# The FFN's first product as seven products of quarters instead of eight

## What is computed

```python
def merge_and_ffn(x, o_attn, o_rwkv, o_fnet, mod, p):
    ...
    x = x + g1 * o
    h = modulate(rmsnorm(x, p['norm_ffn_g']), sh2, sc2)
    gt, up = jnp.split(h @ p['ffn_w_in'], 2, axis=-1)       # (640, 1024) @ (1024, 5632)
    return x + g2 * ((jax.nn.silu(gt) * up) @ p['ffn_w_out'])  # (640, 2816) @ (2816, 1024)
```

## Time and profile before

| | us |
|---|---|
| median of three runs (2017.24 to 2019.22) | 2018.57 |
| the profiled execution | 2016.91 |
| its span, first to last instruction | 2015.1 |
| PE busy | 1912.3 (95%) |
| DVE busy | 804.5 (40%) |
| ACT busy | 634.6 (31%) |
| POOL busy | 517.1 (26%) |
| granted TensorE clock, mean | 0.987 |

### The profile page before, as it was taken

One profiled execution on the slowest core, in us unless ns is written; L12 is line 12 of the kernel. 1 busy time (PEld: TensorE's weight loads), 2 busy tenths in 40 slices (PEclk: granted clock), 3 DMA queues, 4 the chain that ended last, 5 costly groups with the idle time before them and its releaser, 6 DMA issues. The chain is left out here.

```text
span 2015.1 us, 47947 instructions
## 1 busy us (share of the span) xinstructions
PE 1912.3 (95%) x21577; PEld 1789.0 (89%) x21577; DVE 804.5 (40%) x1740; ACT 634.6 (31%) x1254; POOL 517.1 (26%) x251
## 2 busy tenths in 40 slices
PE   5999899899999999999999988989999999999997
PEld 4998588788899999999989866869888999999997
DVE  0522866554243311333153257474525332133322
ACT  3422555552321211212233155455323221111221
POOL 0333400001233333333312340001032333333331
PEclk8999899999999999999999998999999999999999
DMA  9575200002532232222336522000021222332221
GB/s 332 165 203 162 64 4 4 4 5 85 153 100 63 58 99 76 73 71 66 90 102 196 173 67 65 4 2 7 24 64 48 78 64 73 84 84 66 59 65 53
DMA packets 238176, 164.09 MB, mean 81 GB/s; under 512 B 21643, under 2 KB 235381, under 8 KB 237461
## 3 DMA queue, kind: packets, MB, share of 16 engines
q1 hardware_dynamic: 236532, 159.07, 27.1%
q0 software_dynamic: 1440, 1.97, 0.3%
HBM read 157.87 MB, written 3.15 MB: 80 GB/s over the span
## 5 line engine op out<-in xcount | busy, mean ns | idle before, releaser
L669 POOL TENSOR_TENSOR wsplit<-ring,wsplit 128x1024 fp32r<-128x1024 f32 (+1 forms) x134 | 355.4, 2653 | 795.5 <-ACT wsplit L1386 795.5
L873 PE MATMUL PS<-h_hi,wsplit 128*128 128x320 f32 x1408 | 425.6, 310 | 4.4 <-POOL wsplit L669 2.6
L874 PE MATMUL PS<-h_hi,wsplit 128*128 128x320 f32 x1408 | 423.8, 309 | 0.0
L1386 ACT ACTIVATE wsplit<-ring 128x1024 fp32r<-128x1024 f32 (+1 forms) x134 | 152.2, 1136 | 792.2 <-PE PS L874 779.9
L873 PEld LDWEIGHTS PS<-h_hi,wsplit 128*128 128x128 f32 x1408 | 264.2, 188 | 9.1 <-ACT h_hi L1360 4.3
L874 PEld LDWEIGHTS PS<-h_hi,wsplit 128*128 128x128 f32 x1408 | 264.4, 188 | 0.0
L874 PE MATMUL PS<-h_lo,wsplit 128*128 128x320 f32 x704 | 217.1, 309 | 0.0
L873 PE MATMUL PS<-h_lo,wsplit 128*128 128x320 f32 x704 | 217.1, 309 | 0.0
L873 PE MATMUL PS<-hid_hi,wsplit 128*128 128x320 f32 x704 | 213.1, 311 | 0.0
L874 PE MATMUL PS<-hid_hi,wsplit 128*128 128x320 f32 x704 | 212.0, 309 | 0.0
L2032 DVE SCALAR_TENSOR_TENSOR x<-PS,mod,x 128x320 f32<-128x320 f32 x144 | 54.5, 434 | 343.9 <-PE PS L874 343.9
(11 more groups left out here) (383 smaller groups left out, 3728.2 us busy)
## 6 DMA issues: line engine op xcount, KB each, us to landing
ring<-in_w_ada SPq DMA_DIRECT2D x48, 1024.0 KB, 7.6
ring<-in_ffn_w_in SPq DMA_DIRECT2D x88, 512.0 KB, 5.1
ring<-in_ffn_w_out SPq DMA_DIRECT2D x32, 704.0 KB, 4.6
ring<-in_w_in SPq DMA_DIRECT2D x8, 1024.0 KB, 7.4
ring<-in_w_in SPq DMA_DIRECT2D x10, 512.0 KB, 8.8
ring<-in_w_in SPq DMA_DIRECT2D x16, 256.0 KB, 6.5
ring<-in_w_out SPq DMA_DIRECT2D x16, 256.0 KB, 6.8
ring<-in_w_out SPq DMA_DIRECT2D x8, 512.0 KB, 8.0
```

The lines of the kernel that those rows point to most:

```text
L669: nc.gpsimd.tensor_tensor(lo, raw_w, hi, SUB).then_inc(wl_ready(), 1)
L873: mm(lat[:, 0:TH], w, v[:, 0:TH], start=(n == 0), stop=(n == total - 1))
L874: last = mm(cx[:, 0:TH], w, v[:, TH:T], start=(n == 0), stop=(n == total - 1))
L1386: act(hi, raw_w, ACT.Copy).then_inc(wh_ready(), 1)
```

## The change

The first FFN product of one tile is a matrix of 2 x 2 blocks times another: the weights are cut by input half (k-tiles 0 to 3, 4 to 7) and by output (gate, up), h by input half and by tokens (left 320, right 320). The plain way is eight products of quarters, 12 matmuls each. The change makes them by Strassen's algorithm in the Winograd form, seven products of sums of quarters, named by their weight block in the order of computation: A11, A12, S2, S1, S3, S4, A22 (S1 to S4 are sums of the tile's weight blocks). All that is done for 20 of the 22 tiles of a layer (`NFAST`); the first two remain plain.

- The sums of h's quarters (in `h` itself, once a layer) and their high and low parts (`T_hi`, `T_lo`): 4 DVE sums, 4 ACT copies, 4 DVE subtractions of 128 x 1280; and ACT first completes `h` (16 instructions).
- For each fast tile: DVE makes 4 sums of weight blocks (128 x 512), ACT the high part of 7 blocks, DVE the low part of 6, POOL that of A22. There are five slots for blocks: ACT makes the high part five products ahead, DVE the low part four ahead.
- Products gather in PSUM: A11, then S2, S3 and A22 on top of it in a bank of the tile's own (6 or 7); A12 in bank 5, then S1, S4 on top of S1 in the same bank. Between them ACT copies three states out and DVE adds three and multiplies one.
- The FFN is done in four parts of 6, 6, 5, 5 tiles instead of two of 11. An f2 unit is 36 or 30 matmuls; there are 32 a layer instead of 16; its weights come as 256 columns for two units, in three slots.
- The third unit's weights (`FFN0 + 2`) are split with no wait for PE, into `wsplit`.
- SP's load of the last gain waits for the last of the seven-product tiles.
- Buffers lie over others to make room: `Sf` over the recurrence's state, `E4` (which holds `tmp` too) over small tables.

The core of the diff:

```diff
+PARTS = ((0, 6), (6, 12), (12, 17), (17, 22))
+NPLAIN = 2
...
@@ SP
+                    elif old[0] == "f1" and old[1] >= NPLAIN:
+                        e.wait_ge(bl_ready.sem, bl_ready.upto(lo, 6 * (old[1] - NPLAIN + 1)))
+                        e.wait_ge(bp_ready.sem, bp_ready.upto(lo, old[1] - NPLAIN + 1))
...
-            e.wait_ge(acc_ready.sem, acc_ready.upto(DEPTH - 1, ITEM_AT[("up", FT - 1)] + 1))
+            e.wait_ge(sp_done.sem, sp_done.upto(DEPTH - 1, 7 * NFAST))
             e.dma_start(grow, I["norm_final_g"].partition_broadcast(128)).then_inc(ld_grow, 16)
...
@@ POOL
+                for part in range(len(PARTS)):
+                    for si in fast_pairs(part):
+                        n, hi, lo = fast_slot(si, A22)
+                        e.wait_ge(bh_ready.sem, bh_ready.upto(l, 7 * si + A22 + 1))
+                        nc.gpsimd.tensor_tensor(lo, fast_raw(l, si, A22)[1], hi, SUB).then_inc(bp_ready(), 1)
+                    for m in range(KT):
+                        weight_low(UNIT_OF[("f2", m, part)])
...
@@ PE
+                def product(si, q):
+                    n, w_hi, w_lo = fast_slot(si, q)
+                    v_hi, v_lo, _ = fast_in(q)
+                    bank = ps[5] if q in (A12, S1_, S4_) else ps[6 + si % 2]
...
+                    if q == A12 and si >= 1:
+                        e.wait_ge(ps_taken.sem, ps_taken.upto(l, 4 * (si - 1) + 3))
+                    if q in (S2_, S3_, S4_):
+                        e.wait_ge(ps_copied.sem, ps_copied.upto(l, 3 * si + {S2_: 1, S3_: 2, S4_: 3}[q]))
+                    if q in (S1_, A22):
+                        e.wait_ge(ps_taken.sem, ps_taken.upto(l, 4 * si + {S1_: 1, A22: 2}[q]))
+                    for k in range(4):
+                        for p in range(3):
+                            last = mm(bank[:, 0:TH], (w_lo if p == 1 else w_hi)[:, k, :],
+                                      (v_lo if p == 2 else v_hi)[:, k, :],
...
@@ ACT
+                weight_high(FFN0 + 2)
+                for k in range(KT):
+                    e.wait_ge(hl_ready.sem, hl_ready.upto(l, KT + k + 1))
+                    for s, (a, b) in enumerate(STREAMS):
+                        last = act(h[:, k, a:b], h[:, k, a:b], ACT.Identity, bias=mod[:, 24 + k, s:s + 1])
+                    last.then_inc(h_full(), 1)
...
+                    for si in fast_pairs(part):
+                        ends = si == fast_pairs(part)[-1]
+                        own_x, tile = ps[6 + si % 2], si + NPLAIN - PARTS[part][0]
+                        e.wait_ge(hid_split.sem, hid_split.upto(l, max(NPLAIN, si + 1)))
+                        product_copy(si, A11, E1[si % 2], own_x)
+                        block_ahead(si, A11, 5)
+                        block_ahead(si, A12, 5)
+                        left_or_right_sigmoid(si, 1, E1[si % 2])
+                        e.wait_ge(hid_split.sem, hid_split.upto(l, NPLAIN + si))
+                        product_copy(si, S2_, E2, own_x)
+                        block_ahead(si, S2_, 5)
+                        product_copy(si, S1_, G5[:, :], ps[5])
+                        block_ahead(si, S1_, 5)
+                        if ends:
+                            weight_high(f2)
+                        block_ahead(si, S3_, 5)
+                        block_ahead(si, S4_, 5)
+                        left_or_right_sigmoid(si, 3, E2)
+                        block_ahead(si, A22, 5)
+                        e.wait_ge(ps_taken.sem, ps_taken.upto(l, 4 * si + 4))
+                        act(hid_hi[:, tile, 0:TH], E1[si % 2], ACT.Copy)
+                        e.wait_ge(right_ready.sem, right_ready.upto(l, si + 1))
+                        act(hid_hi[:, tile, TH:T], E2, ACT.Copy).then_inc(hid_high(), 1)
...
@@ DVE
+                def block_low(si, q):
+                    if q == A11:
+                        weight_sum(si, S1_)
+                        weight_sum(si, S2_)
+                    if q == S3_:
+                        weight_sum(si, S4_)
+                    n, hi, lo = fast_slot(si, q)
+                    e.wait_ge(bh_ready.sem, bh_ready.upto(l, 7 * si + q + 1))
+                    V.tensor_tensor(lo, fast_raw(l, si, q)[1], hi, SUB).then_inc(bl_ready(), 1)
+                    if q == S1_:
+                        weight_sum(si, S3_)
...
+                for k in range(KT):
+                    e.wait_ge(h_full.sem, h_full.upto(l, k + 1))
+                    if k == 3:
+                        input_sum(quarter(0, 0), quarter(0, 1), quarter(0, 0))
+                        plain_gate(0)
+                input_sum(quarter(0, 1), quarter(1, 1), quarter(0, 1))
+                plain_up(0)
+                input_sum(quarter(1, 1), quarter(1, 1), quarter(0, 0))
+                input_sum(quarter(1, 0), quarter(1, 0), quarter(1, 1))
+                block_low(0, 0)
+                sum_low(S2_)
+                sum_low(S1_)
+                block_low(0, 1)
+                block_low(0, 2)
+                plain_gate(1)
+                sum_low(S3_)
+                sum_low(A22)
+                plain_up(1)
+                block_low(0, 3)
+                for part in range(len(PARTS)):
+                    for si in fast_pairs(part):
+                        own_x, tile = ps[6 + si % 2], si + NPLAIN - PARTS[part][0]
+                        left = E1[si % 2]
+                        if si > fast_pairs(part)[0]:
+                            pair_low(si - 1, tile - 1)
+                        low_ahead(si, A11)
+                        e.wait_ge(ps_copied.sem, ps_copied.upto(l, 3 * si + 1))
+                        product_sum(si, A12, left, ps[5], ADD)
+                        low_ahead(si, A12)
+                        e.wait_ge(g_sig.sem, g_sig.upto(l, 2 * si + 1))
+                        own.after(V.tensor_tensor(left, left, F4, MUL))
+                        low_ahead(si, S2_)
+                        low_ahead(si, S1_)
+                        e.wait_ge(ps_copied.sem, ps_copied.upto(l, 3 * si + 3))
+                        product_sum(si, S3_, G5[:, :], own_x, ADD)
+                        low_ahead(si, S3_)
+                        product_sum(si, S4_, E2, ps[5], ADD)
+                        low_ahead(si, S4_)
+                        e.wait_ge(g_sig.sem, g_sig.upto(l, 2 * si + 2))
+                        own.after(V.tensor_tensor(E2, E2, F4, MUL))
+                        product_sum(si, A22, left, own_x, MUL)
+                        V.tensor_tensor(E2, E2, G5[:, :], MUL).then_inc(right_ready(), 1)
+                        low_ahead(si, A22)
+                    pair_low(si, tile)
+                    for m in range(KT):
+                        residual(("f2", m, part), m, 40, TH)
```

More of the change, by code:

```diff
@@ L54, in chunk_order @@
         ffn = []
[L55 to L56 removed]
+        for part, (a, b) in enumerate(PARTS):
+            ffn += [(l, "f1", i) for i in range(a, b)] + [(l, "f2", 4 * part + m) for m in range(KT // 2)]
         order += ffn[:1] + ahead[6:] + ffn[1:]
@@ L88, in split_units @@
     u += [(("out", m), ("wo", m // 2), m % 2, KT) for m in range(KT)]
[L89 to L92, removed]
+    for i in range(NPLAIN):
+        u += [(("gate", i), ("f1", i), 0, KT), (("up", i), ("f1", i), 1, KT)]
+    for part, (a, b) in enumerate(PARTS):
+        u += [(("f2", m, part), ("f2", 4 * part + m // 2), m % 2, b - a) for m in range(KT)]
     return u
@@ L120, in item_order @@
     o += [("out", m) for m in range(KT)] + [("inv", 1)]
[L121 to L124, removed]
+    for i in range(NPLAIN):
+        o += [("gate", i), ("up", i)]
+    for part in range(len(PARTS)):
+        o += [("f2", m, part) for m in range(KT)]
     return o
@@ L217, in state_plan, with fast_pairs, part_of @@
     return plan
+A11, A12, S2_, S1_, S3_, S4_, A22 = range(7)
+T_AT = {S2_: 0, S1_: 1, S3_: 2, A22: 3}
+def fast_pairs(part):
+    a, b = PARTS[part]
+    return range(FAST[part], b - NPLAIN)
+def part_of(si):
+    return [p for p in range(len(PARTS)) if si in fast_pairs(p)][0]
 class Signal:
@@ L1302, in _ @@
                     ada_cols(3, ahead)
-                for u in range(FFN0 + 2, NUNIT):
-                    name = UNITS[u][0]
+                for u in range(FFN0 + 2, FFN0 + 2 * NPLAIN):
                     whole(u)
-                    if name[0] == "f2" and name[2] == 1 and name[1] > 0:
-                        if ahead:
-                            norm_part(ahead, 0, name[1] - 1)
-                        else:
-                            last_part(name[1] - 1)
+                for part in range(len(PARTS)):
+                    for si in fast_pairs(part):
+                        for q in range(7):
+                            product(si, q)
+                    for m in range(KT):
+                        whole(UNIT_OF[("f2", m, part)])
+                        if part == len(PARTS) - 1 and m > 0:
+                            if ahead:
+                                norm_part(ahead, 0, m - 1)
+                            else:
```

(9 more changed lines are left out.)

275 lines of the change are left out of this document (216 added, 59 removed).

## The result

The changed kernel takes 1999.32 us (1998.34 to 2003.56), the kernel before beside it 2018.89 (2017.24 to 2019.47): a ratio of 0.9908, 95% interval 0.9891 to 0.9926. The forecast was 2004.0 and "faster"; the medians differ by 19.6. The profiled execution has a span of 1996.9 us, 18.2 less than before; the sum had 14.6 less.

The account below looks back on a forecast made before the run. PE bound the old kernel; in the new one a round of waits was to set the tile's time. Two layers at -6.7 (-13.4) and the tail's -1.2 gave -14.6 us: median 2018.6 to 2004.0, range 1994 to 2013.

Parts of the forecast that it names:

- the tail: End of the kernel: the last gain's load, issued earlier, no longer holds the output; -1.2 us.
- Matmuls: First FFN product: 480 matmuls fewer at about 0.147 us each, worth 70.4 us if nothing else bound.
- Rival (4): Fast tiles: 12 matmuls in a row into one bank are slower, 2035 to 2050 us; chance 0.08 together with (3).
- The loop: Fast tiles following another: closed round of waits among PE, DVE and ACT takes 13.72 us, against 12.32 of PE work.
- First tiles of the parts: First tiles of parts 2 to 4: splits are ready, only A11's copy is late by 0.4; 12.80 us each.
- The start's stall: Start of each layer's FFN: PE waits 4.3 us before S2, which starts at 588.6; that tile costs 16.7.
- the removed wait: Third weight split, start of stage: no longer waiting for PE gains nothing, as POOL delays DVE's low parts; +0.3 us.
- Rival (5): Half clock behind the start's stall, 1.8 us a layer, left out of the sum; chance not in the text given.
- (1): Fast tiles PE-bound: the loop closes in less than 12.32 us, -62, giving 1956; chance 0.17 including a halfway case at 1985.
- (2): Slower loop, over 14.18 us; with each of twelve steps 0.05 longer it is 14.32, giving 2023 us; chance 0.17.
- (3): POOL's operation falls into the loop: +1.3 us for each of 32 tiles, 2046; chance 0.08 together with Rival (4).
- f2 is covered: Second FFN product: its shorter units still cover residuals and splits; cost 0 to 0.2 us for each part.

Follow-up runs that it names:

- The version in which only the loop is freed: Changed kernel with ACT's split of the next tile's S3 block moved behind the two copies into hid_hi; 1965.59 us, ratio 0.9733 to the kernel before.
- the version with two moves: Changed kernel with ACT's S3 split behind the copies and the low halves of S3's and A22's inputs moved into the first fast tile; 1956.19 us, ratio 0.9691.
- the changed kernel again: The changed kernel timed and profiled a second time without edits, as reference for the follow-up runs; 2001.55 us, ratio 0.9907 to the kernel before.
- the version with the split behind the sigmoids: Changed kernel with the third weight split waiting for PE again, but issued behind ACT's first two sigmoids; 1999.95 us, ratio 0.9915 to the kernel before.

## Why the prediction was right

**The sum closes.** By stage: the FFN of layer 0, from the low parts of h to the reciprocal of the next norm, went from 470.36 to 462.69 us, -7.7 (predicted -6.7); that of layer 1, to the last reciprocal, from 476.47 to 467.18, -9.3 (predicted -7.9 with the tail). The other 1.2 of the 18.2 lie in stages that the change doesn't touch.

**Matmuls.** 480 fewer, every 0.147 us, 12 in a row into one bank at 1.76 (603.51 plus 1.76 plus a wait of 0.38 and 0.07 to restart is 605.72). Rival (4) is out. The row was right. The estimate by the formula of the Trainium skill (TensorE: Matmul & The Clock Gate, Wait — 56ns, not 53.3ns?), 135.8 ns, is not met here either.

**The loop.** Predicted 13.72 by a sum of ten terms, measured 13.60. Step by step, with the predicted value in brackets: PE and back to DVE 7.38 (7.40), right half and S1 low to S3's sum 1.41 (1.43), to ACT 0.78 (0.73), split 0.54 (0.54), copies and handover 0.84 (0.94), two low halves 0.82 (0.82), S4 sum and S3 low 1.20 (1.22), A12 sum and handover 0.63 (0.64). Most of the difference is in the copies, where I put 0.10 for the handover behind the second one's end and 0.03 were due. 32 x 0.12 = 3.8 us less than predicted. The two waits were put at 0.8 and 0.45 and are 0.75 and 0.38. That this chain, and no load, makes the time is shown from both sides: 0.66 us in it cost 0.67, beside it nothing, and with one split moved the tile is 12.42, PE's work within 0.1.

**First tiles of the parts** were to cost 12.80; the first one of part 2 takes 12.60 (A11 at 682.26 to A11 at 694.86): -1.2 for six.

**The start's stall.** Predicted 4.3 with S2 at 588.6; measured 4.29, S2 at 588.89, of which 0.42 is the later arrival of the whole stage (its low parts begin at 554.32, before at 553.90). POOL stretched these to 9.65 us (7.50 before), 2.15 more where I had 2.3. The second tile starts at 566.91, or 566.49 on the clock of before, against 566.44: the removed wait came back as predicted, as 0.05 and not 0.3.

**What the sum left out.** Rival (5), half clock behind the stall, came true: I named it, priced it at 1.8 us a layer and left it out of the sum as small. It took 1.5: from S2 to the next S2 are 14.62 us where 12.32 and a wait of 0.75 make 13.07. In layer 1 it is 14.68. In the second profiled execution of the same kernel the low level lasted longer and took 2.5 and 2.1 us, so this term is not even the same from one execution to the next. So the parts are -3.8 for the loop, -1.2 for the first tiles, -0.5 for the second tile's start, +3.1 for the clock: -2.4, and FFN stages 17.0 shorter against 14.6. Four small errors of both signs; the forecast was as near as it was partly since they cancel.

**The removed wait.** "Gains nothing" was right about what I compared, the start of the second tile before and after. It was wrong as a price: in the changed kernel the wait is worth 9 us. Its worth was read from the kernel before, where little stood behind it in ACT's queue. The change itself puts sixteen writes and the head of a 24 us chain behind it.

**Rivals.** (1) was the bigger prize. The version in which only the loop is freed takes 1965.59, not the 1956 given for a PE-bound loop: its tile is 12.42 instead of 12.32, and half clock behind the stall takes another 4.3 us in the two layers. That the version with two moves takes 1956.19 is in part a coincidence, since it also has a shorter stall. Still, about 62 us are there, and the order of two queues decides on them. (2) did not occur: no step took over 0.05 more than its rows gave. I had held the loop for firm at nine DVE and three ACT steps; one of the three did not belong there. (3) did not occur: POOL starts at 605.90, 0.33 after the end of the A12 sum, where I had 0.3, and what it blocks is a product that has time. f2 is covered: its residuals come every 5.28 us (645.50, 650.78, 656.07) and PE has no wait there. In the tail the output no longer waits for the last gain.

## What to carry to other kernels

When work is cut to a bottleneck's bare minimum, write out the closed round of who waits for whom before counting loads: here the loads fitted with room, and the round was 1.3 us a tile longer than PE's work. In each engine's queue, put ahead what closes the round and behind it what only has to be ready later; one such line was worth 36 us, nearly twice the whole change as it was made. And price a wait by what the new kernel queues behind it, not by what the old one did.

## What the runs showed of the hardware

- Behind every stall of 4.06 to 4.30 us at S2 (eight versions, both layers) PE ran at 1.2 GHz, for 3 to 6 us: until 592 from a restart at 588.9, until 593.8 from 588.3, until about 596 from 590.35 in the changed kernel again. Behind stalls of 1.3 to 2.5 us in the FFN it stayed at 2.4 GHz. In the version with the split behind the sigmoids 3.10 us in layer 0 left the clock high and 3.22 in layer 1 did not, for 3.3 us. Such a stall costs 1.2 to 2.8 us more than it shows, the same stall different amounts in different executions; what decides on the amount is not shown. Nor is the length of the gap all: in the mixing part of the kernel before the clock falls to 0.50 at 243.7 us, with no gap of PE longer than 2.13 us in the 50 us ahead of it.
- DVE and POOL: an operation of DVE with two SBUF inputs that meets a POOL operation waits for its end and then takes 0.35 (320 columns) or 0.54 us (512), so 1.47 in place of 0.49 and 1.67 in place of 0.69. Between two POOL operations in a row DVE gets one of its own done, and the second costs it 0.98 where it lasts 1.43.
- A handover from ACT to DVE costs almost nothing behind the end of ACT's operation (616.19 + 0.45 to 616.67), and ACT starts 0.78 us after the start of a DVE sum that takes 0.69.
